# Third mixer: GpSimd splits the first output weight piece after it has scaled the differential outputs, and VectorE reads the compressed keys, values and scores earlier in its order

## The reference, cut to what matters

```
o_diff = diff_attention(dq, dk, dv, lam)                       # 4 heads, two softmaxes each
o_diff = rms_norm_2(o_diff, diff_subln) * (1.0 - lam_init)
...
kc = compress_tokens(kc_tok, tok_idx, k_pos, k_w1, k_w2)       # 15 blocks of 32 tokens
vc = compress_tokens(vc_tok, tok_idx, v_pos, v_w1, v_w2)
sc = einsum('bghqd,bgnd->bghqn', qb, kc) * scale
pc = masked_softmax(sc, cmp_end <= qpos)
o_cmp = einsum('bghqn,bgnd->bghqd', pc, vc)
...                                                            # o_slc and o_win: 8 heads over all tokens
return gate0 * o_cmp + gate1 * o_slc + gate2 * o_win
...
return concatenate([o_diff, o_nsa], axis=-1) @ w_out
```

## Time and profile before

| what | value |
|---|---|
| three runs | 900.82 us median, 900.64 to 901.08 |
| the profiled execution | 899.98 us, span 898.2 us |
| TensorE busy | 883.8 us, 98% of the span |
| VectorE busy | 691.8 us, 77% |
| ScalarE busy | 289.5 us, 32% |
| GpSimd busy | 297.8 us, 33% |
| mean granted TensorE clock | 0.997 of full |
| bytes moved | 160.23 MB, 178 GB/s on average |

### The profile page before, as it was taken

The page is one execution under the profiler, slowest core; times in us unless marked ns, Lnnn a source line. Parts: engine busy times, 40 slices in busy tenths (PEclk is TensorE's granted clock), DMA queues, the critical chain, the costliest instruction groups (busy, mean ns, idle before and its releaser), DMA issues.

```text
span 898.2 us, 12926 instructions
## 1 busy us (share of the span) xinstructions
PE 883.8 (98%) x4851; PEld 743.1 (83%) x4851; DVE 691.8 (77%) x731; ACT 289.5 (32%) x567; POOL 297.8 (33%) x205
## 2 busy tenths in 40 slices
PE   9999999999999999999999999999999999999997
PEld 7987798888887787788888888888767988888885
DVE  6699888777777775889777778778578887776775
ACT  6648271111112501354111111554676541111112
POOL 2230223444434432213444443331152223333331
PEclk9999999999999999999999999999999999999999
DMA  8960627555558265216655555366043376555541
GB/s 283 337 231 1 234 98 234 190 191 196 193 223 289 82 202 188 93 68 232 219 192 194 192 204 169 124 236 219 16 189 96 102 239 221 187 186 188 187 163 47
DMA packets 82263, 160.23 MB, mean 178 GB/s; under 512 B 5080, under 2 KB 40426, under 8 KB 82224
## 3 DMA queue, kind: packets, MB, share of 16 engines
q1 hardware_dynamic: 82208, 159.69, 51.8%
q10 hardware_dynamic: 16, 0.00, 0.0%
HBM read 158.63 MB, written 1.05 MB: 178 GB/s over the span
## 4 chain that ended last, share of the span: by engine, by line
PE 88%; DMA 4%; ACT 3%; DVE 2%; POOL 1%; issue 1%; SPq 0%; DVEq 0%; POOLq 0%; ACTq 0%
PE ps L2165 84%; PE ps L2169 3%; DMA raw<-in_even_w_in 2%; DMA raw<-in_odd_w_pw 2%; ACT arena L1665 1%; ACT arena L2057 1%; POOL w_hi L636 0%; DVE arena L1499 0%; ACT arena L1853 0%; DVE w_lo L864 0%; POOL st L675 0%; POOL st L751 0%; DVE x_res L957 0%; DVE st L1495 0%; POOL st L674 0%
## 5 line engine op out<-in xcount | busy, mean ns | idle before, releaser
L864 DVE TENSOR_TENSOR w_lo<-raw,w_hi 128x2048 fp32r<-128x2048 f32 (+2 forms) x134 | 308.9, 2328 | 38.9 <-POOL w_hi L845 21.8
L2165 PE MATMUL ps<-act_hl,w_hi 128*128 128x512 f32 (+1 forms) x1088 | 241.2, 367 | 0.6 <-POOL w_hi L658 0.2
L2165 PEld LDWEIGHTS ps<-act_hl,w_hi 128*128 128x128 f32 x1088 | 182.4, 189 | 30.0 <-issue 1.0
L2165 PE MATMUL ps<-w_hi,act_hl 128*128 128x512 f32 (+3 forms) x656 | 180.9, 382 | 1.2 <-DVE w_lo L864 0.8
L2165 PE MATMUL ps<-w_hi,hl 128*128 128x512 f32 (+1 forms) x648 | 178.3, 388 | 0.0
L651 POOL TENSOR_SCALAR w_hi<-raw 128x2048 fp32r<-128x2048 f32 x48 | 119.0, 2480 | 149.6 <-PE ps L2165 138.7
L2165 PEld LDWEIGHTS ps<-w_hi,act_hl 128*128 128x128 f32 x656 | 118.6, 188 | 25.2 <-issue 3.5
L2165 PEld LDWEIGHTS ps<-w_hi,hl 128*128 128x128 f32 x648 | 119.2, 188 | 23.3
L2165 PEld LDWEIGHTS ps<-act_hl,w_lo 128*128 128x128 f32 x960 | 129.2, 191 | 8.2
L2165 PE MATMUL ps<-act_hl,w_lo 128*128 128x256 f32 x960 | 132.3, 282 | 0.0
L636 POOL TENSOR_SCALAR w_hi<-raw 128x2048 fp32r<-128x2048 f32 (+2 forms) x22 | 50.0, 2276 | 163.9 <-PE ps L2165 111.2
(11 more groups left out here) (241 smaller groups left out, 825.4 us busy)
## 6 DMA issues: line engine op xcount, KB each, us to landing
raw<-in_mlp_w SPq DMA_DIRECT2D x64, 1024.0 KB, 5.2
raw<-in_w_gate SPq DMA_DIRECT2D x22, 512.0 KB, 3.9
raw<-in_w_up SPq DMA_DIRECT2D x22, 512.0 KB, 4.9
raw<-in_w_down SPq DMA_DIRECT2D x11, 1024.0 KB, 5.0
raw<-in_odd_w_pw SPq DMA_DIRECT2D x16, 512.0 KB, 6.2
raw<-in_w_in SPq DMA_DIRECT2D x8, 1024.0 KB, 6.1
raw<-in_even_w_in SPq DMA_DIRECT2D x4, 1024.0 KB, 12.3
raw<-in_even_w_out SPq DMA_DIRECT2D x4, 1024.0 KB, 5.7
```

The costliest lines, as they stand in the source:

```text
L864: tt(w_lo[slot_of(n)][:, 0:w], raw[slot_of(n)][:, 0:w], w_hi[slot_of(n)][:, 0:w].bitcast(F32), ALU.subtract).then_inc(S("w_split"), pieces ...
L2165: return pe.matmul(o, l, r, start=start, stop=stop, skip_group_check=True)
```

## The change

Two orders are changed, and no instruction is added or removed. On GpSimd the wait for `w_hi` and the copy of the first output weight piece go from ahead of the compressed probabilities to behind the scaling of the differential outputs. On VectorE `compressed_kv` goes ahead of `row_max(DH + 1)`, and `compressed_shift` goes ahead of `weigh(DH + 1)`.

```
@@ GpSimd
                 ins.then_inc(S("kcv"), 1)
-                cursor[0] = FIRST["w_out_2"]
-                gp.wait_ge(S("w_hi"), cursor[0])
-                hi_until(FIRST["w_out_2"])
                 gp.wait_ge(S("cscores_read"), 1)
                 me.link(gp.memset(pcm, 0.0))
...
                 for i in range(8):
                     ins = gp.tensor_scalar(od[:, i, :], od[:, i, :], rs8[:, i:i + 1], None, ALU.mult)
                 ins.then_inc(S("o_normed"), 1)
+                cursor[0] = FIRST["w_out_2"]
+                gp.wait_ge(S("w_hi"), cursor[0])
+                hi_until(FIRST["w_out_2"])
                 gains_product(3, 9)
@@ VectorE
                 compressed_hidden()
+                compressed_kv()
                 row_max(DH + 1)
-                compressed_kv()
+                compressed_shift()
                 weigh(DH + 1)
-                compressed_shift()
                 row_max(DH + 2)
```

## The result

The changed kernel takes 903.03 us (median of 11 runs, 902.23 to 905.79), against 900.82 before (11 runs, 899.63 to 903.13): a ratio of 1.0025, 95% interval 1.0014 to 1.0037, or 2.2 us slower. That is 0.8 us above the predicted 902.2 and within the range.

What follows compares the result with a forecast made beforehand. TensorE, busy 98% of the span, was taken as the bound, with ScalarE from 661 to 669 us. Gain -0.5 and hold +1.87 make +1.4, added to the 900.82 median: 902.2 us; 8-in-10 range 900.0 to 904.0.

Steps and rivals of the forecast that it cites:

- three signs that the prediction names as wrong: L698 starting behind that L1495 or itself held; granted clock below 1.00 behind 676; gain at 659 lost before 664.
- The gain: Third mixer's attention: scores read 1.57 us sooner, transposes of `DH` no longer wait for L1515; 0.5 us gained (0.3 to 0.6).
- VectorE reads keys and values sooner: VectorE before the small products: waits 1.2 us, copies at the same time as before, gains nothing; row maxima 1.7 us later.
- The hold: Before the transposes of `DH + 5`: L698 holds VectorE's L1495, so they start 1.87 us later, less the 0.5 gain.
- the forecast +1.4: Whole kernel: -0.5 gain and +1.87 hold make +1.4 on the profiled execution; median 902.2, chance 0.41.
- rival 1: TensorE's clock also falls behind the 2.6 us gap before the transposes of `DH + 5`: 1.4 us more, 903.6; chance 0.28.
- Rival 4: Low TensorE clock at 657.5 goes away, up to 1.4 us back: 900.8 with L1495's stall, 898.9 without; chance 0.05.
- The rule weighed: Skill's rule: L1499, scaling within SBUF, stops for all of L698; by the rows it loses only a few tenths.
- Rival 2: VectorE's L1495 gets in before L698 (margin 0.18 us), L1499 runs beside L698, only the gain stands: 900.3; chance 0.17.

Runs made afterwards that it cites:

- experiment 4: The changed kernel run again without edits: 903.77 us against 901.03 before, ratio 1.0040.
- experiment 2: Kernel before with only GpSimd's weight copy moved, VectorE's order as before: 903.49 us against 901.03, ratio 1.0027.
- experiment 5: Changed kernel plus eight bf16 products on TensorE in the gap before the transposes of `DH + 5`: 901.86 us against 901.28 before, ratio 1.0007.
- experiment 1: Kernel before with only VectorE's two moves, GpSimd's order as before: 900.88 us against 901.03, ratio 1.0000; repeated, 901.25 against 900.19, ratio 1.0002.
- experiment 3: Changed kernel with GpSimd's gain product L698 waiting until all twelve heads are weighed: 900.67 us against 901.03 before, ratio 0.9991; repeated, 900.11 against 901.28, 0.9989.
- experiment 6: Changed kernel with GpSimd's gain product L698 put ahead of the weight copy L636: 903.76 us against 901.28 before, ratio 1.0026.
- experiment 8: Changed kernel with late gain product, and weight copy waiting until L1495 of `weigh(DH + 5)` is done: 902.19 us against 900.19 before, ratio 1.0023.
- experiment 7: Kernel before with VectorE's two moves and gain product after all weighings: 899.57 us against 901.28, ratio 0.9984; repeated, 901.91 against 900.19, 1.0007.

## Why the prediction was right, and where it was short

**The mechanism was the forecast one.** GpSimd's copy, moved behind the scalings, pushes the gain product L698 onto VectorE's L1495 of `weigh(DH + 5)`, which is held until L698 ends; TensorE stands still for it. Both parts alone, and the product taken out, say so. But two of the three signs that the prediction names as wrong did appear in the changed kernel's profiles: the clock fell behind 676, and the gain at 659 was lost before 664. And 903.03 lies above the 902.6 from which the prediction calls the kernel slower, which it gave 0.37, against 0.58 for no change. That the median came within 0.8 us of 902.2 is in part luck: experiment 4, the same kernel, is 3.6 us slower than before, and the changed stretch is 3.47 us longer in both profiles. A caution of the prediction, that L1495 might slip in first with a margin of 0.18 us, did not come true in any profile of a kernel in which L698 followed the copy: L698 was ahead by 0.16 to 0.18 us in two (experiments 2 and 5) and by 0.75 in the two of the changed kernel.

**VectorE reads keys and values sooner: right.** It waits 1.20 us, as was worked out, and gains nothing. ScalarE's later exponentials are hidden by its idling.

**The gain: right in size, where it is there.** The 0.5 us came out as 0.58 in experiment 1. GpSimd's part does not add to it: L1495 of `weigh(DH + 5)` comes 17.89 us behind the start of the small products with VectorE's part alone (experiment 1), 17.88 with both parts (experiments 3 and 5), 18.13 with GpSimd's alone and 18.47 before. In both profiles of the changed kernel itself, though, it comes 19.21 and 19.03 us behind, for a reason that follows below.

**The hold: right in size.** Experiment 5, where only the hold is left, gives +1.27 us, against the forecast +1.4.

**The term that was too small was the clock.** The forecast took rival 1 for the less likely (0.28 against 0.41). In four of the five profiles with a gap of 2 us that nothing filled, TensorE's clock fell behind it, and the stretch from the transposes of `DH + 5` to the projection took 8.3 to 8.5 us in place of 6.9: 1.4 to 1.6 us, what rival 1 was priced at. The measured +2.2 us (1.3 to 3.3 by its interval) lies between the forecast (+1.4) and rival 1 (+2.8); the second set, +3.6 (0.0040 of 900.8), is nearer to the rival. I had taken from the stretch of 661 to 669, with its many short waits, that the clock holds; it did not tell what happens behind one gap of 2 us. That the five profiles stand for the mean of all executions was not shown. The mean granted clock of all executions doesn't settle it either. In one set it is 0.9959 over the 12 runs of experiment 6 and 0.9974 over the 12 of experiment 5, and 3.4 us at the lower level make a difference of 0.0019; but it is 0.9956 over the 35 runs of the kernel before, which has no such gap.

**The profile shows 3.47 us and not 2.8** because of one more thing, which the prediction did not have. The low clock behind the small products lasted about 3.4 us before, but about 6.8 us in both profiles of the changed kernel (657.9 to 664.7 above) and in experiment 6. The transposes of `DH` then came 4.40, 4.12 and 4.15 us behind the start of the small products, against 3.54 in experiment 5, where the low stretch was short, and 4.18 before: the gain was gone. TensorE's transposes of `DH + 5` came 21.93, 21.74 and 21.75 us behind, against 21.17 in experiment 5. The parts add up: 1.27 us as in experiment 5, 0.76 for the longer low stretch and 1.44 for the low clock behind the gap make 3.47 (1.27, 0.57 and 1.63 in experiment 4). This is also why the margin at L1495 was 0.75 and not 0.18: the longer low stretch holds back VectorE's part of the chain more than GpSimd's, and the hold gets shorter, 1.6 in place of 2.2 us. Whether it lasts short or long was not the change's doing as far as I can tell: experiments 3, 5 and 8 have the same code up to that point; their profiles have it short, and the second one of experiment 3 has no low clock at all. What decides it stays open.

**Rival 4's price was wrong.** In no profile of the changed kernel was the low clock behind the small products gone. It was gone in the second profiles of experiments 1, 3 and 7, and there the way was the same as in the first ones (26.20, 26.02 and 26.01 us), not 1.4 us shorter.

**The rule weighed.** The Trainium skill (SBUF — State Buffer, Who interferes with whom) says that a `tensor_scalar` within SBUF can enter a mode with both port pairs, and that it is then blocked for the whole of a GpSimd instruction that came first. Experiment 8 agrees with it (2.64 us against 1.01, one scaling of 1.92 us), and the reading of the earlier trace rows, a few tenths lost and no more, was wrong for a long instruction. Beside L828, whose instructions are 0.6 us from start to start, the four lost only 0.2 us; how the rule and this measurement go together stays open. Rival 2's escape, that L1499 would run beside L698, was most likely not open: the scalings were tested under the copy, not under L698 itself.

## What to carry to other kernels

Where GpSimd and VectorE both work in SBUF, ask of each GpSimd instruction which VectorE instructions it will meet, not whether its result is in time: this copy had 9 us of slack, and moving it cost 2 us through its neighbour. A long GpSimd instruction belongs where VectorE works from PSUM (beside the copy L1515 took its usual 0.47 us) or is idle, or behind a wait that puts it past the chain; one such wait took the loss away. And a gap on TensorE can cost about twice what it adds when the clock falls behind it (here 1.3 us for hold less gain, and 1.4 to 1.6 behind it), so it is to be priced with the work that follows.

## What the runs showed of the hardware

- A low clock can be free. From the small products to the projection the kernel with the late product took 26.02 us with the clock low for some 3.4 us in it, and 26.02 with the clock at 1.00 throughout: there ScalarE was the limit (busy 7.88 of 7.88 us). Experiments 1 and 7 have such a pair too (26.20 and 26.20, 26.01 and 26.01). Where it was low for about 6.8 us, L1495 of `weigh(DH + 5)` came 1.15 to 1.33 us later than in experiment 5, and 0.57 to 0.76 of that was left behind the hold. Behind the gap of `DH + 5`, where TensorE is the limit, 3.4 us of it cost 1.4 to 1.6.
- The granted clock differs between executions of the same code. Gaps of 2.06 and 2.65 us were followed by a fall, one of 2.23 was not, and behind the small products it was low for 3.4 us, for 6.8 us, or not at all. What decides it was not found.
- The runs of one kernel spread over 3 to 5 us. Much of this lies ahead of the changed stretch: in the thirteen profiles the small products start between 654.67 us, where TensorE did not wait for the high part of the first weights (L658), and 658.64, where it waited 2.5 us for it and its clock was then low from about 12.3 to 15.8 us.
- Totals can mislead: two sets of one kernel differed by 0.23% in their ratio (0.9984 and 1.0007), while its way through the changed stretch was the same to 0.01 us in both profiles. For changes of half a microsecond such a distance between two fixed points of the trace tells more than the total, if the clock is looked at with it.
